# Ordering the second down projection: ordinary half panels and block products in a two-block kernel

## What is computed

```
h2 = rms_norm(x, norm2_g[l])
x = x + (jax.nn.silu(h2 @ w_gate[l]) * (h2 @ w_up[l])) @ w_down[l]
```

## Time and profile before

| | us |
|---|---|
| median of 3 runs | 802.62 |
| lowest and highest run | 802.52, 802.87 |
| the profiled execution, its own time | 802.98 |
| span of the profiled execution | 801.5 |

### The profile page before, as it was taken

How to read it: one execution, slowest core, us unless ns; L and a number is a source line. 1 busy time by engine, 2 the same in 40 slices (tenths; PEclk the granted TensorE clock), 3 DMA queues, 4 the chain that set the end, 5 groups by cost and what they waited for, 6 DMA issues and landing times. The chain is left out here.

```text
span 801.5 us, 13178 instructions
## 1 busy us (share of the span) xinstructions
PE 795.6 (99%) x5164; PEld 696.8 (87%) x5164; DVE 625.1 (78%) x1035; ACT 457.2 (57%) x738; POOL 90.7 (11%) x77
## 2 busy tenths in 40 slices
PE   8999999999999999999999999999999999999998
PEld 6888888999898888899999998887778888888886
DVE  6888989785555766679999997486866898787977
ACT  6667677554535544456656563466665566555552
POOL 0001000010011302101101110011100333011100
PEclk9999999999999999999999999999999999999999
DMA  9654564557432555475687656464424666884331
GB/s 317 187 166 157 176 229 145 151 146 228 123 118 88 172 173 199 167 237 180 193 251 244 224 186 209 165 203 160 156 79 147 198 207 214 288 282 161 107 103 54
DMA packets 118125, 144.09 MB, mean 180 GB/s; under 512 B 11552, under 2 KB 86704, under 8 KB 117808
## 3 DMA queue, kind: packets, MB, share of 16 engines
q1 hardware_dynamic: 115616, 141.22, 54.7%
q10 hardware_dynamic: 2448, 2.03, 1.0%
HBM read 141.78 MB, written 1.46 MB: 179 GB/s over the span
## 5 line engine op out<-in xcount | busy, mean ns | idle before, releaser
L1754 DVE TENSOR_TENSOR panel_lo<-panel_raw,panel_hi 128x1024 fp32r<-128x1024 f32 x237 | 300.8, 1272 | 106.8 <-ACT panel_hi L1236 105.1
L652 PE MATMUL bank<-x_halves,panel_hi 128*128 128x256 f32 (+1 forms) x1536 | 367.0, 322 | 0.7 <-DVE x_halves L2222 0.7
L1236 ACT ACTIVATE panel_hi<-panel_raw 128x1024 fp32r<-128x1024 f32 (+1 forms) x239 | 252.2, 1057 | 152.9 <-PE bank L652 150.8
L652 PE MATMUL bank<-x_halves,panel_lo 128*128 128x256 f32 x1024 | 288.3, 282 | 0.0
L652 PEld LDWEIGHTS bank<-x_halves,panel_hi 128*128 128x128 f32 x1536 | 255.8, 190 | 23.3 <-issue 0.9
L652 PEld LDWEIGHTS bank<-x_halves,panel_lo 128*128 128x128 f32 x1024 | 195.0, 190 | 0.2
L652 PE MATMUL bank<-panel_hi,x_halves 128*128 128x512 f32 x384 | 122.1, 399 | 0.0
L652 PEld LDWEIGHTS bank<-panel_hi,x_halves 128*128 128x128 f32 x384 | 70.0, 188 | 14.4 <-DVE panel_lo L1754 0.6
L652 PE MATMUL bank<-panel_lo,x_halves 128*128 128x512 f32 x192 | 75.1, 391 | 0.0
L652 PE MATMUL bank<-panel_hi,act_hi 128*128 128x512 f32 x156 | 60.9, 390 | 0.2 <-DVE panel_lo L1754 0.2
L652 PE MATMUL bank<-panel_hi,act_lo 128*128 128x512 f32 x156 | 60.7, 389 | 0.0
(11 more groups left out here) (312 smaller groups left out, 1017.1 us busy)
## 6 DMA issues: line engine op xcount, KB each, us to landing
panel_raw<-in_w_in SPq DMA_DIRECT2D x35, 1024.0 KB, 5.3
panel_raw<-in_w_up SPq DMA_DIRECT2D x30, 1024.0 KB, 5.4
panel_raw<-in_w_down SPq DMA_DIRECT2D x16, 1024.0 KB, 5.0
panel_raw<-in_w_gate SPq DMA_DIRECT2D x10, 1024.0 KB, 5.4
panel_raw<-in_w_out SPq DMA_DIRECT2D x8, 1024.0 KB, 5.0
panel_raw<-in_w_in SPq DMA_DIRECT2D x11, 512.0 KB, 4.7
panel_raw<-in_w_branch_fox SPq DMA_DIRECT2D x4, 1024.0 KB, 5.0
panel_raw<-in_w_branch_gdn SPq DMA_DIRECT2D x4, 1024.0 KB, 5.0
```

What stands on the lines that cost most here:

```text
L652: return e.matmul(o, l, r, start=start, stop=stop, skip_group_check=True)
L1236: return e.activation(o, i_, ACT.Copy, scale=scale)
L1754: e.tensor_tensor(lo, raw_view(i, k0, kt), hi.bitcast(F32), ALU.subtract).then_inc(s_lo, 1)
```

## The change

Only the table GROUP_ORDER changes:

```diff
-GROUP_ORDER = [("b11", None, "b21", None, "b22", None, "t3", None, "t1", None, "t2", None, "t4", None),
-               ("b11", None, "b21", None, "b22", None, "t3", None, "t1", "t2", None, "t4", None, None)]
+GROUP_ORDER = [(None, None, "b11", None, "b21", None, "b22", None, "t3", None, "t1", None, "t2", None, "t4"),
+               ("b11", None, "b21", None, "b22", "t3", None, "t1", None, "t2", "t4", None, None)]
```

## The result

The changed kernel takes 804.75 us (median of 8 runs, 804.32 to 806.94), the kernel before 802.57 us (median of 8 on the same chip, 802.27 to 803.33): 2.2 us more. The ratio is 1.0032, with a 95% interval of 1.0022 to 1.0041. The forecast was 804.4 us, with a range of 803.0 to 805.3.

A forecast was written before the change was run, and what follows sets the result against it. PE, busy 99% of the span, was taken to bound the kernel. The terms -0.47 + 1.32 + 0.96 = +1.81 us on the profiled 802.98 gave 804.8, as a median 804.4 us, range 803.0 to 805.3.

The forecast's parts named there:

- Part 1: Ahead of the stage's eighth step: PE's existing stall goes because that step is due one block product later; -0.47 us.
- Part 2: Group 1, b22 beside t3: DVE's split for the next ordinary half comes late and PE waits there; +1.32 us.
- the walk: Following DVE and ACT through group 1: DVE idles about 1.6 us for ACT's copy of b22, queued behind p1's.
- Part 3: End of the kernel: DVE's sums behind t2 no longer hide under PE, so the last bank starts later; +0.96 us.
- Rival 2: One of the two new waits, in group 1 or at the end, is hidden: 803.1 or 803.5 us; chance 0.18.
- Rival 3: Faster: DVE stays ahead in group 1 and at the end, and the old stall goes: 802.15 us; chance 0.12.
- rival 4: Worse: late addition or bunched outputs, 804.9 to 805.5 us (0.07), or halved PE clock, up to 819 (0.01).

The follow-up runs named there:

- e7: Kernel before, with the last product of the up projection's tail done by DVE right behind its silu instead of by POOL: 802.14 us, ratio 0.9995.
- e10: Kernel before, with eight one-column memsets more at the very start of DVE's program: 802.11 us, ratio 0.9990.
- e2: Kernel before, with only group 1 reordered so that block product t3 stands next to b22 and two ordinary halves follow: 802.83 us, ratio 1.0002.
- e3: Changed kernel, with an ordinary half again between block products b22 and t3 of group 1: 803.49 us, ratio 1.0010.
- e4: Changed kernel, with ACT's copy of bank p1 to sum_u two iterations later: 803.15 us, ratio 1.0005.
- e9: Changed kernel, with the left columns' two output transfers copying constants without waiting for their result; DVE's work stays: 804.79 us, ratio 1.0024.
- e1: Kernel before, with only the end of group 1 reordered so that block product t2 stands next to t4: 803.73 us, ratio 1.0014.
- e5: Changed kernel, with the end of group 1 put back to the old order: 803.32 us, ratio 1.0010.
- e6: Changed kernel's group 0; group 1 with a half between b22 and t3 and the old end; ACT's copy of p1 two iterations later: 801.98 us, ratio 0.9993.
- e8: Kernel before, with the first three banks' output transfers held until the third bank is added: 803.63 us, ratio 1.0020.

## Why the prediction was right, and where it was not

**The sum.** Forecast +1.81 us, measured +2.01 in the traces and +2.18 in the medians, inside the range. The three terms came out at -0.47, +1.33 and +1.12, against -0.47, +1.32 and +0.96, so the sum is not owed to errors that cancel.

**Part 1, the old stall: -0.47.** It went, as forecast. The changed kernel started N5's split at 755.23, 12.46 us after the stage's first matmul, against 754.97 - 1.27 = 753.70 forecast, 12.82 after it. It was 0.36 sooner because the idle 0.46 us of the earlier trace rows was not there; I had carried it along. What I named as the cause was half of it: POOL's product is one (e7: 0.05 us left), but all of the wait but 0.11 us also goes when only DVE's instruction stream shifts by eight places (e10). Each of the two had to be there for N4 to start 0.36 us late, and the removal of neither needs an ordinary half in front. The gain that the change could have was available without it.

**Part 2, N11: +1.32.** Measured 0.15 + 0.11 at t3 and 0.96 + 0.11 at N11, 1.33 in all; only the division between the two was different, for I had put all of it at N11. DVE's time sets N11's start, so what PE loses at t3 is not lost again there. The cause holds as the walk had it: e2 and e3 show that one missing half leaves 0.26 us and two leave 1.33, and e4 that the idle time behind ACT's copy of p1 is what makes them count. The rival by which DVE is simply overloaded fell with e4.

**Part 3, the end: +0.96.** Measured +1.12, and this term was mis-sized in both pieces. DVE's lateness was 0.81, not 0.96: its chain from the first block sum to line 2083 took 802.33 - 795.65 = 6.68 us and not 6.85, by the three additions of line 2089, 1.98 us from the first's start to line 2083 where I had counted 2.15 to their end. And the last transfer took 0.3 us longer, which I had left out of the sum and kept as an upper bound of 0.4. Of the earlier banks' transfers, which I had named for that bound, the left columns' two have no part in it (e9); the third bank's transfer is the only one left that leaves nearer to the last, 0.78 us ahead in e9 where it was 1.48 before (798.16 for a last one at 799.64). That this nearness is the cause was not tried alone.

**The rivals.** Rival 2 (one of the costs hidden) is excluded by e1 and e5, which show each cost alone, 1.1 and 0.8 us over before (the latter with the old stall gone). Rival 3 would have needed N11's split 1.2 us sooner; e6 is a kernel without either cost, and its -0.53 us is, with e10's -0.52, the most that any run gained. Of rival 4, the clock did not fall at the new waits: after N11's the granted clock stays at 1.00, the 2.4 GHz level, in the changed kernel's window (us, busy times with counts, then granted clock, DMA share, GB/s):

```profile
786.21:801.32 15.11, 15.11 (x66) 12.31 (x66) 12.47 (x15) 3.55 (x4) 0.00 (x0) 1.00 0.00 0
```

The matmuls there are 0.23 us apart but for N11's second. The fall that the Trainium skill ("TensorE: Matmul & The Clock Gate", Part 1) describes after an idle stretch did not follow on this wait, so leaving it out of the sum was right here.

## What to carry to other kernels

Here DVE waited for ACT, and ACT's queue held a copy that waited for DVE. Such a loop costs nothing as long as a third engine, here PE, has enough work, and shows when the order of that engine's work changes. So walk the queues in program order, with starts taken from the trace, before trading places of long and short products. Judge an order of steps by what each engine has in hand ahead of each product, and by how much remains behind the last reduction: here the new order saved 0.5 us ahead of step 8 and cost 1.3 and 1.1 us elsewhere. A stall of half a microsecond may hang on an accident; move or drop a cheap neighbour (e7, e10) before rearranging a stage for it.

## What the runs showed that was not expected

- DVE's 0.46 us of idle time for nothing stood at the same addition in every kernel that kept group 0's old order and DVE's instruction count ahead of it (before, e1, e2, e7, e8), and eight one-column instructions, 700 us sooner, removed it and 0.36 us of the stage.
- The clock did fall elsewhere in the changed kernel's profiled execution: its mean was 0.56 between 11 and 14 us, near the 1.2 GHz level, and 0.80 between 14 and 16, behind waits of PE of 1.64 us (line 778) and 0.66 us. The stretch kept 1.00 in the traces with a wait of 0.39 (before), 1.19 (e4) and 1.31 us (e5) at line 778, so what decides it stays open. With the 0.7 us of "issue" it put the stage 1.9 us later, nearly as much as the whole change; the span of a single profile was no guide to it.
- Sending 1 MB of output in one bunch at the end cost 1.05 us by itself, more than three times the 0.3 us expected (e8).
